# A transformer stack on one core: the opening's weight order and first modulated norm, by quarters

## The reference

```python
cond = jax.nn.silu(c)
for l in range(DEPTH):                       # DEPTH = 2
    mod = cond @ ada_w[l] + ada_b[l]         # 1024 x 9216
    sh1, sc1, g1, sh2, sc2, g2, sh3, sc3, g3 = jnp.split(mod, N_MOD, axis=-1)
    h = rms_norm(x, norm_ffn1[l]) * (1.0 + sc1[:, None]) + sh1[:, None]
    x = x + 0.5 * (1.0 + g1)[:, None] * ((silu(h @ ffn1_w1[l]) * (h @ ffn1_w3[l])) @ ffn1_w2[l])
    ...
```

## Time and profile before

| | before |
|---|---|
| median of 3 runs | 2802.19 us |
| lowest and highest | 2797.94, 2802.31 us |
| the profiled execution | 2800.25 us, span 2798.4 us |
| TensorE busy | 2747.1 us, 98% of the span |
| VectorE, ScalarE busy | 2094.7 us (75%), 1480.9 us (53%) |
| HBM read | 516.94 MB, 185 GB/s over the span |

### The profile page before, as it was taken

The page is one execution under the profiler, slowest core; times in us unless marked ns, Lnnn a source line. Parts: engine busy times, 40 slices in busy tenths (PEclk is TensorE's granted clock), DMA queues, the critical chain, the costliest instruction groups (busy, mean ns, idle before and its releaser), DMA issues.

```text
span 2798.4 us, 53534 instructions
## 1 busy us (share of the span) xinstructions
PE 2747.1 (98%) x22658; PEld 2460.5 (88%) x22658; DVE 2094.7 (75%) x3300; ACT 1480.9 (53%) x2030; POOL 138.4 (5%) x257
## 2 busy tenths in 40 slices
PE   6999999999999999999999999999999999999999
PEld 6888899998888898998988988889888988898888
DVE  7987767789878877677886687755776677668874
ACT  3545754665455467446554466544654455436653
POOL 1000000200000000002000040000100000004000
PEclk9999999999999999999999999999999999999999
DMA  9775327548768752474685525555465557551553
GB/s 310 250 253 181 110 93 241 182 151 269 261 208 270 255 168 93 136 224 155 195 274 183 182 76 181 185 177 181 134 198 181 183 172 230 183 184 63 184 189 109
DMA packets 517006, 521.44 MB, mean 186 GB/s; under 512 B 16551, under 2 KB 513776, under 8 KB 516768
## 3 DMA queue, kind: packets, MB, share of 16 engines
q1 hardware_dynamic: 514160, 517.32, 57.5%
q0 software_dynamic: 816, 0.27, 0.1%
q10 hardware_dynamic: 1792, 0.44, 0.1%
HBM read 516.94 MB, written 1.05 MB: 185 GB/s over the span
## 4 chain that ended last, share of the span: by engine, by line
PE 91%; DVE 5%; ACT 2%; issue 1%; DMA 1%; POOL 0%; ACTq 0%; DVEq 0%
PE P L66 89%; PE P L69 2%; DVE wsp L75 1%; DVE arena L83 1%; ACT wsp L72 1%; DVE arena L75 1%; ACT arena L72 1%; DVE ACC L83 0%; DVE HX L83 0%; DMA raw<-in_ada_w 0%; DMA arena<-in_norm_ffn 0%; POOL arena L80 0%; DVE arena L89 0%; DVE X L95 0%; ACT HX L72 0%
## 5 line engine op out<-in xcount | busy, mean ns | idle before, releaser
L66 PE MATMUL P<-HX,wsp 128*128 128x512 f32 (+1 forms) x9920 | 1531.2, 315 | 10.4 <-DVE wsp L75 5.3
L66 PEld LDWEIGHTS P<-HX,wsp 128*128 128x128 f32 x9920 | 1381.1, 190 | 141.1 <-issue 12.6
L75 DVE TENSOR_TENSOR wsp<-raw,wsp 128x2048 fp32r<-128x2048 f32 (+4 forms) x454 | 947.3, 2090 | 282.4 <-ACT wsp L72 281.3
L72 ACT ACTIVATE wsp<-raw 128x2048 fp32r<-128x2048 f32 (+4 forms) x454 | 793.5, 1750 | 475.5 <-PE P L66 401.2
L66 PE MATMUL P<-FG,wsp 128*128 128x256 f32 (+1 forms) x2816 | 497.0, 337 | 0.0
L66 PEld LDWEIGHTS P<-FG,wsp 128*128 128x128 f32 x2816 | 428.4, 188 | 63.3 <-DVE wsp L75 1.2
L72 ACT ACTIVATE arena<-P 128x512 f32<-128x512 f32 (+3 forms) x375 | 208.3, 571 | 476.6 <-PE P L66 452.0
L75 DVE TENSOR_TENSOR arena<-arena,P 128x512 f32<-128x512 f32 (+2 forms) x226 | 147.0, 652 | 160.4 <-ACT arena L72 135.9
L83 DVE SCALAR_TENSOR_TENSOR ACC<-raw,sm,ACC 128x256 f32<-128x256 f32 x476 | 230.9, 485 | 16.8
L66 PE MATMUL P<-GX,wsp 128*128 128x256 f32 (+1 forms) x1592 | 229.3, 303 | 0.8 <-DVE GX L75 0.8
L66 PEld LDWEIGHTS P<-GX,wsp 128*128 128x128 f32 x1592 | 209.9, 190 | 14.2 <-issue 1.5
(11 more groups left out here) (119 smaller groups left out, 1490.7 us busy)
## 6 DMA issues: line engine op xcount, KB each, us to landing
raw<-in_ffn_w SPq DMA_DIRECT2D x120, 1024.0 KB, 5.4
raw<-in_ada_w SPq DMA_DIRECT2D x72, 1024.0 KB, 5.1
raw<-in_w_in SPq DMA_DIRECT2D x52, 1024.0 KB, 5.2
raw<-in_ffn_w_gate SPq DMA_DIRECT2D x44, 1024.0 KB, 5.4
raw<-in_ffn_w_up SPq DMA_DIRECT2D x44, 1024.0 KB, 5.3
raw<-in_ffn_w_down SPq DMA_DIRECT2D x32, 1024.0 KB, 4.9
raw<-in_nsa_w_in SPq DMA_DIRECT2D x20, 1024.0 KB, 5.4
raw<-in_ffn_w SPq DMA_DIRECT2D x16, 768.0 KB, 4.2
```

What stands on the lines that cost most here:

```text
L66: return self if self.e is None else self.e.matmul(*a, skip_group_check=True, **k)
L72: return self if self.e is None else self.e.activation(*a, **k)
L75: return self if self.e is None else self.e.tensor_tensor(*a)
```

## The change

The first two split units, `f1` 0 and `f3` 0, are planned ahead of the eight `ada` parts and are split as soon as ScalarE has squared x. The parts now alternate: even j is a quarter of the scale and is reduced on VectorE, odd j is a quarter of the shift and is multiplied on TensorE. For each quarter q the halves of x times gain go into `XB` and the shift's two columns beside them (`high_act`, `low_dve`, `shift_pair_*`), and TensorE multiplies two chunks of both units with them (`chunks_early`), with the 64 matmuls of the next odd part between the chunks of `f3` 0. Steps 0 to 2 of this FFN work on `XB` and are scaled by the root afterwards; h itself is made after step 1 for steps 3 and on. The fills of the first FFN move to steps 2, 4, 5, 6, 8, 9, 10 and one more behind an `f2` unit. Rope and the turned rows move from step 3 to step 7. Row block 0 is issued by SP behind x; all other small transfers are issued by POOL after `mod` part 7.

```diff
         def part_of(j):
             x = j % 36
+            if j < 8:
+                return j // 2 if j % 2 else 4 + j // 2
...
-            return j < 8 and j % 2 == 0
+            return j < 8 and j % 2 == 1
...
-                if ada and (i in (2, 3, 4, 6, 7, 8, 10) if f else i % 4 != 3 and i < 10):
+                if f == i == 0:
+                    plan_ada(8)
+                elif ada and (i in (2, 3, 4, 6, 7, 8, 10) if f else i in (2, 4, 5, 6, 8, 9, 10)):
                     plan_ada(1)
...
-                    if ada and (s == 0 or f and s == 2 and q == 0):
+                    if ada and (s == 0 or s == 2 and q == 0):
...
-        plan_ada(8)
...
+        def start_pool(e):
+            e.wait_ge(*AMOD.at(7))
+            e.dma_start(posi, A["positions"].rearrange("o s -> (o s)").partition_broadcast(128)).then_inc(*pos_in.up("pos", 16))
+            for t in range(1, nrow):
                 rows_dma(e, t)
...
         def early(n):
 
-            return 1 <= n < 6
+            return n < 6
...
+        def first_act(e):
+            u = U["f1", 0][0]
+            ready_act(e, u, u + 1)
+            for q in range(4):
+                high_act(e, 0, 2 * q)
+                high_act(e, 0, 2 * q + 1)
+                if q == 0:
+                    root_act(e, 0)
+                shift_pair_act(e, q)
+                if q == 1:
+                    e.wait_ge(*NSPR.at(0))
+                    e.activation(RE, P[bank["nspr", 0]][:, 0:256], ACT.Copy).then_inc(*NR_.up(0))
+            ready_act(e, U["ada"][7], U["f1", 0][1])
+
+        def first_dve(e):
+            u = U["f1", 0][0]
+            square_dve(e, 0, 1)
+            square_dve(e, 0, 2)
+            ready_dve(e, u, u + 1)
+            for q in range(4):
+                ready_dve(e, U["ada"][2 * q], U["ada"][2 * q])
+                mod_dve(e, 2 * q)
+                low_dve(e, 0, q)
+                if q == 0:
+                    root_dve(e, 0)
+                mod_dve(e, 2 * q + 1)
+                shift_pair_dve(e, q)
+            ready_dve(e, U["ada"][7], U["f1", 0][1])
+
+        def first_pe(e):
+            us = [U["f1", 0][0], U["f3", 0][0]]
+            sums_pe(e, 0)
+            ada_pe(e, 0)
+            ada_pe(e, 1)
+            ps = [take2(e, (k, 0, 0)) for k in ("f1", "f3")]
+            for q in range(4):
+                chunks = (2 * q, 2 * q + 1)
+                chunks_early(e, us[0], ps[0], 0, chunks)
+                if q < 3:
+                    b = take(e, ("ada", 2 * q + 3))
+                    chunks_early(e, us[1], ps[1], 0, chunks, lambda i: fresh_pe(e, 2 * q + 3, b, i // 2, range(4 * (i % 2), 4 * (i % 2) + 4)))
+                    give(("ada", 2 * q + 3), AMOD.at(2 * q + 3))
+                    ada_pe(e, 2 * q + 2)
+                else:
+                    chunks_early(e, us[1], ps[1], 0, chunks)
+                if q == 0:
+                    spread_pe(e, 0)
...
         def ffn_pe(e, f, n):
             for i in range(NB):
-                if i == 3 and f == 0:
-                    for t in range(3, nrow):
+                if i == 7 and f == 0:
+                    for t in range(1, nrow):
                         turn_rows(e, t)
...
-                        if early(n) and i == 1 and k == "f1":
+                        if n == 0 and i < 3:
+                            chunks_early(e, u, p, 0, range(8))
+                        elif early(n) and i == (1 if n else 3) and k == "f1":
                             lins(e, [u], [p], HX, h_pairs(n))
...
+                if f == 0 and i == 1:
+                    norm_act(e, 0, U["f3", f][i])
...
         def sync_program(e):
             e.dma_start(C[:, 0:256], cst[:, 0:256]).then_inc(*c_in.up("c", 16))
             e.dma_start(xin, A["x"].rearrange("o (t p) d -> p (o t) d", p=128)).then_inc(*x_in.up("x", 16))
+            rows_dma(e, 0)
...
-            for j in (0, 2, 1, 4, 3, 6, 5, 7):
-                ada_pe(e, j)
```

More of the change, by code:

```diff
@@ L520, in lins, with chunks_early @@
                     chunk_of(e, u, p, X2, kk)
+        def chunks_early(e, u, p, n, kks, between=None):
+            wh, wl, k, _ = halves(u)
+            e.wait_ge(*LO.at(u))
+            for kk in kks:
+                e.wait_ge(*HLO.at(("x", n, kk // 2)))
+                if n == 0:
+                    e.wait_ge(*HLO.at(("x", 0, "shift", kk // 2)))
+                for m in range(2):
+                    s = slice(m * 128, m * 128 + 128)
+                    ins = three(e, tile_of(p, m)[:, 0:258], wh[:, kk, s], wl[:, kk, s], XB[:, 0, kk, :], XB[:, 1, kk, :], kk == 0, kk == 7)
+                    if between is not None:
+                        between(2 * (kk - kks[0]) + m)
+            if kks[-1] == 7:
+                ins.then_inc(*MM.up(u))
         def lins_early(e, us, ps, n):
             def chunks_of(i, kks):
[L526 to L534, removed]
+                chunks_early(e, us[i], ps[i], n, kks)
             e.wait_ge(*HLO.at(("x", n, "shift")))
@@ L658, in rows_dma @@
             st = ar(17152 + t * 128, 128)
-            e.wait_ge(*SET.at("rows"))
+            e.wait_ge(*SET.at("rows" if t else "row"))
             for base, c0, ap in prow[t][0]:
@@ L767, in fill_pe, with fresh_pe @@
                 ada_pe(e, nada[u])
+        def fresh_pe(e, j, b, q, ks):
+            u = U["ada"][j]
+            w = landed(u)
+            e.wait_ge(*RAW[u % NR].at(u))
+            e.wait_ge(*COND_.at("cond"))
+            for k in ks:
+                for x in range(2):
+                    ins = e.matmul(P[b][half(x), q:q + 1], w[:, k, 128 * q + 64 * x:128 * q + 64 * x + 64], COND[:, k:k + 1],
+                                   start=k == 0, stop=k == 7)
+            if q and ks[-1] == 7:
+                ins.then_inc(*AMM.up(j))
         def ada_pe(e, j):
@@ L772, in ada_pe @@
             if fresh(j):
-                w = landed(u)
-                e.wait_ge(*RAW[u % NR].at(u))
-                e.wait_ge(*COND_.at("cond"))
                 for q in range(2):
[L777 to L780, removed]
+                    fresh_pe(e, j, b, q, range(8))
             else:
@@ L811, in mod_dve @@
             q, w = x // 12, (x // 4) % 3
-            if x % 4 == 3 and w:
+            if j < 8 and w:
+                e.wait_ge(*AMOD.at(j))
+                c = 2 * (x - 4)
+                g = pcols["n10"] + c
+                e.scalar_tensor_tensor(ABS[0][:, c:c + 2], MODS[0][:, 8 + c:10 + c], 1.0, PC[:, g:g + 2],
+                                       ALU.add, ALU.mult).then_inc(*AMOD.up(("part", 0, 1, x - 4)))
+            elif x % 4 == 3 and w:
                 e.wait_ge(*AMOD.at(j))
@@ L826, in mod_ready @@
         def mod_ready(l, part):
-            return AMOD.at(36 * l + part_of(4 * part + 3)) if part % 3 == 0 else AMOD.at(("part", l, part))
+            if l == 0 and part < 2:
+                return AMOD.at(("part", 0, 1, 3) if part else 7)
+            return AMOD.at(36 * l + 4 * part + 7) if part % 3 == 0 else AMOD.at(("part", l, part))
         SQ = ar(0, 8, 256)
@@ L945, in norm_act @@
                 root_act(e, n)
-            if early(n):
+            if early(n) and n:
                 e.wait_ge(*NSPR.at(n))
@@ L1069, in unscaled_next, with begun_act, begun_dve, on_x @@
             return late(n + 1) or early(n + 1)
+        def begun_act(e, f, i, u):
+            if f or i:
+                ready_act(e, u)
+            else:
+                ready_act(e, U["ada"][7], U["f3", 0][1] if u == U["f1", 0][0] else None)
+        def begun_dve(e, f, i, u):
+            if f or i:
+                ready_dve(e, u)
+            else:
+                ready_dve(e, U["ada"][7], U["f3", 0][1] if u == U["f1", 0][0] else None)
+        def on_x(n, i):
+            return early(n) and i < (1 if n else 3)
         def ffn_act(e, f, n):
             for i in range(NB):
-                if i == 3 and f == 0:
+                if i == 7 and f == 0:
                     rope_act(e)
-                    for t in range(3, nrow):
+                    for t in range(1, nrow):
                         turned_act(e, t)
@@ L3173, in vector_program @@
             start_dve(e)
-            u = behind(-1)
-            for j in range(8):
-                mod_dve(e, j)
-                ready_dve(e, U["ada"][j], U["f1", 0][0] if j == 7 else U["ada"][7])
+            first_dve(e)
             for l in range(2):
-                norm_dve(e, 3 * l, u)
+                if l:
+                    norm_dve(e, 3 * l, u)
                 ffn_dve(e, 2 * l, 3 * l, (l, 0))
```

115 lines of the change are left out of this document (53 added, 62 removed).

## The result

The changed kernel takes 2821.64 us (median of 4 runs, 2819.30 to 2823.87), the kernel before 2802.24 us (4 runs, 2797.94 to 2802.31). The ratio is 1.0075 with a 95% interval of 1.0062 to 1.0087: the change costs 19 us, where +7.5 was forecast. The profiled execution of the changed kernel took 2823.87 us (span 2822.1), 23.6 us more than the profiled one before; it is the slowest of the four, so sums made on the two traces come out some 4 us above the difference of the medians.

A forecast was written before the change was run, and what follows sets the result against it. It took TensorE as the bound, so only its dense stream's start and interruptions counted. Terms 6.0 + 1.6 + 0.6 + 0.3 = +8.5 us on 2800.25 gave 2808.8; with half of 1.9 added, 2809.7 us, range 2801 to 2818.

The forecast's parts named there:

- S0 = 29.5: Opening: TensorE's first dense matmul at 29.5 us instead of 44.13, a gain of 14.6 us.
- D = 2.9 us: End of each quarter: latency through VectorE and ScalarE to the shift's low half, TensorE idle, 2.9 us.
- A to C: Quarter's TensorE work: A `f1` chunks; B `f3` chunks with odd part; C even part. Full pace 1.5, 4.1, 0.5 us.
- I take half pace for A and half of B in the first quarter and full pace after.: Clock in the four quarters: low only early in the first, +2.3 us; otherwise 9.0 us a quarter.
- Rival 2: Quarters: clock stays low or falls in each pause; +17.6 us, 2818 to 2820, or about 2814; chance 0.21.
- S3: Start of the last quarter's dense matmuls, forecast at 58.8 us.
- Step 7, +0.3: Rope and turned rows moved from step 3 to step 7: same cost plus two more rows, +0.3 us.
- Three matmuls for two, +1.6: Steps 1 and 2: three matmuls of 258 columns instead of two of 512 and 256, +0.8 us each.
- the stall at the split of `f3` 3, +0.6: VectorE, loaded with the moved norm, reaches this split about 0.6 us late; 0 to 2.
- the cover of 4.0: Wait for the split of unit `f1` 1, 4.0 us, under which the last quarter's 24 matmuls (3.1) should end.
- The small transfers: POOL issues some 41 from 58 us on; nobody waits for them before step 7; no cost counted.

The follow-up runs named there:

- mid_part: Changed kernel with part 1 ahead of part 0 and each even part's eight matmuls after half of the odd part's 64; one run, 2816.12 us.
- pause_filled: Changed kernel plus 12 dense matmuls that nobody reads in the pause behind each of the first three quarters; ratio 1.0061 to the kernel before.
- fresh_block: Changed kernel with each odd part's 64 one-column matmuls in one block behind the quarter's 24 dense ones; ratio 1.0056 to the kernel before.
- even_first: Changed kernel, step 7 copies before rotary tables, part 1 before part 0, quarters ordered 24 dense, even part, odd part; ratio 1.0001 to the kernel before.
- turn_first: Changed kernel with ScalarE copying the five turned row blocks before the rotary tables in step 7; ratio 1.0052 to the kernel before.
- small_late: Kernel before with only small transfers late (row block 0 behind x) and row blocks and rotary tables in step 7, copies first; ratio 0.9985.
- small_late_tables_first: Against small_late: rotary tables ahead of the copies of the five turned row blocks in step 7; one run, 2806.91 us.

## Why the prediction was wrong

- *The start, S0 = 29.5.* Measured 28.94. TensorE had x at 6.49, the silu of c and the squares followed as counted, part 0's matmuls came at 24.16 (25.0 less their own time was forecast), part 1's stood behind them. Right.
- *The latency D = 2.9 us.* From the end of the even part's matmuls to the next dense one: 52.71 to 55.23, 2.5 us. Right within 0.4, and mid_part showed the chain to be what it is.
- *The price of A to C at either level.* 12.4 us at half pace was forecast, D among them, 13.1 measured: the weight load waits 0.23 us in front of each of the four groups of one-column matmuls (the row at 47.47), which makes 0.9, and D was 0.4 shorter. The sum at half pace had no term for these changes of form; at full pace I had chosen 0.4 for eight. At full pace pause_filled shows 8.9 to 9.7 with the extra work's share in it, for 9.0. Right in size.
- *"I take half pace for A and half of B in the first quarter and full pace after."* This is the step that failed. The clock was at 0.50 in all of the first two quarters and most of the third. The three took 37.1 us instead of 29.3: +7.8 us. I had seen that dense work lifts the pace within 3 us (rows 7), and that one-column matmuls don't. But the change puts only 15 dense matmuls in a row ahead of a mixed stretch and a pause. With 24 in a row (fresh_block) the clock rose each time, and it fell again in each quarter; even_first, which only reorders, brings the three quarters to 23.8 us. Rival 2 described this, with S3 near 67 and the trace's figures of half pace; it had 0.21. That 66.00 comes so near is in part luck: the same opening gave 68.81 in turn_first.
- *Step 7, +0.3.* This failed too: five banks held through the rotary work cost 4.95 us of pause and 1.7 us of low clock behind it, with 1.2 us of transposes and wait in front of the step 7.9 us, against about 1.3 in step 3 before: +6.6. I had read from rows 5 what three row blocks cost and scaled it by two more transposes of 0.1 us, without counting banks. With three the pause came in front of step 4, with five in front of the second half of step 7.
- *Three matmuls for two, +1.6; the stall at the split of `f3` 3, +0.6.* The 192 matmuls of steps 1 and 2 took 23.6 us where 24.4 were forecast, so three for two cost +0.9 (192 in 23.22 us at full pace in pause_filled); the stall didn't come (no wait for a split in steps 1 to 3), which its range of 0 to 2 allowed. The last quarter's 24 matmuls ran at half pace, 5.2 us, and so outlasted the cover of 4.0: +1.2, as in rival 2.
- *The small transfers.* As forecast, nobody waited for them. What they had cost where they stood before was not in the sum of the old opening, and small_late put it at 2.3 us of the stream.

The sum on the traces up to the mark: 8.5 forecast, -0.6 at the start, +7.8 in the quarters, -0.3 in steps 0 to 3 (1.16 less 0.83 and 0.6), +6.3 in step 7 (6.6 less the 0.3 forecast) make 21.7; measured 22.4, and 0.7 are left unplaced. A further 1.3 us of the spans' difference falls behind the mark, in stages that the change doesn't touch; the twelve traces differ there by up to 5.3 us. Two terms of the sum were at fault, and each of them is a loss of the clock or of a resource, not a duration misread. The range's upper end (2818) took in only the near end of rival 2; the low clock and the held banks together were in no case.

The prediction had named a rule of the Trainium skill (page "TensorE: Matmul & The Clock Gate", section "HAM oscillation — how this bites in real kernels"): bursts with waits between them start slow again. The traces agree in that the bursts started slow again, fresh_block's three times 5.50 us most plainly; but here TensorE was idle for only 2.2 to 2.5 us between them, with one-column matmuls ahead, and in even_first, with 0.79 us idle, 24 dense ones still took 4.55. The forecast had said that no row showed it and had gone by full pace.

## What to carry to other kernels

Count a burst's matmuls at the pace of the clock that it will meet: a start that is made earlier by cutting dense work into pieces with thin work and waits between them can run at half pace for all of its length. Put the dense matmuls in one row and hide the latency of the next piece behind the thin ones. When turned or staged tiles are put ahead of a stage, count the PSUM banks they hold until the copying engine comes to them, and put the copies ahead of that engine's long work. And before a single trace is taken as proof of an edit, look whether the difference begins where the edit does: pause_filled's first quarter was shorter ahead of its first extra matmul.

## What the runs showed of the hardware

- The clock reacts to the kind of work: 3.6 us of one-column matmuls with TensorE busy all the time left it at 0.50 (64 in 3.58 us), and by the end of 24 dense ones in a row it was up in all three quarters of fresh_block. Extra matmuls whose result nobody reads made the second quarter 3.4 us shorter (pause_filled). Behind the transposes of x it was up: the 64 one-column matmuls right behind them took 2.03 us in small_late (the row at 10.54), all later ones there 3.58.
- A pause of 4.95 us in the middle of dense work lowered it: 96 matmuls in 18.78 us instead of 17.1, in the changed kernel and, with 4.74 us and 18.91, in small_late_tables_first.
- The table by windows can show 1.00 for stretches that run at half pace, probably where they lie ahead of the first change in the record. In other kernels the same opening, with the same durations, is shown at 0.50 (25 to 30 us: 1.00 in pause_filled, 0.50 in turn_first; 64 one-column matmuls in 3.58 us in both). The durations are the safer sign.
